# Hybrid mLSTM and attention layer, one core: x loaded between the first weight pieces, its squares between the weight copies, tile bursts issued in two parts, and u modulated and partly split on GpSimd

## What is computed

```python
mod = silu(cvec) @ w_ada + b_ada                 # cvec is c for latent tokens, c_ctx for the prompt
shift, scale, gate = split(mod, 3)               # each 2048 wide
u = rmsnorm(x, norm_pre_w) * (1 + scale) + shift
p = u @ w_in                                     # then attention, mLSTM, merge, output projection
```

## Time and profile before

| | us |
|---|---|
| median of 3 runs | 2286.16 (2285.41 to 2289.83) |
| the profiled execution, its own time | 2288.56 |
| span of the profiled execution | 2287.0 |
| TensorE busy, share of the span | 2138.0, 93% |
| VectorE busy | 875.2, 38% |
| ScalarE busy | 701.8, 31% |
| GpSimd busy | 105.2, 5% |
| end of the start (last matmul of the tiles steps) | 188.8 |

### The profile page before, as it was taken

The page is one execution under the profiler, slowest core; times in us unless marked ns, Lnnn a source line. Parts: engine busy times, 40 slices in busy tenths (PEclk is TensorE's granted clock), DMA queues, the critical chain, the costliest instruction groups (busy, mean ns, idle before and its releaser), DMA issues.

```text
span 2287.0 us, 34161 instructions
## 1 busy us (share of the span) xinstructions
PE 2138.0 (93%) x13450; PEld 1984.5 (87%) x13450; DVE 875.2 (38%) x1666; ACT 701.8 (31%) x1094; POOL 105.2 (5%) x184
## 2 busy tenths in 40 slices
PE   3898999899999999999999899999999899989995
PEld 1458999899999998999899899898989899977774
DVE  4775555432224233222322234342433533342223
ACT  4763111233233223322322223232323533331221
POOL 1001000000000000000000000000000100000000
PEclk7999999999999999999999999999999999999998
DMA  6873655542233223222422426243444534413223
GB/s 248 272 235 108 198 171 170 175 114 80 83 107 89 78 77 110 86 82 73 117 79 82 128 64 141 76 110 121 99 133 95 172 120 120 123 60 120 74 73 128
DMA packets 295167, 274.00 MB, mean 120 GB/s; under 512 B 17921, under 2 KB 243961, under 8 KB 292641
## 3 DMA queue, kind: packets, MB, share of 16 engines
q1 hardware_dynamic: 282416, 218.21, 33.6%
q0 software_dynamic: 12656, 54.40, 6.5%
HBM read 232.65 MB, written 39.92 MB: 119 GB/s over the span
## 4 chain that ended last, share of the span: by engine, by line
PE 83%; DVE 7%; issue 3%; ACT 2%; DMA 2%; SPq 1%; DVEq 0%; POOL 0%; ACTq 0%; POOLq 0%
PE bank L1374 60%; PE bank L1598 9%; PE bank L1463 2%; PE bank L1289 2%; PE bank L1345 2%; PE bank L1513 2%; PE bank L1328 1%; PE bank L1504 1%; DMA WORK<-in_state_n_dram 1%; PE bank L1515 1%; PE bank L1436 1%; DMA Y<-in_x_prompt_dram 1%; DVE WL L858 1%; DVE WL L876 1%; DVE XL L1246 1%
## 5 line engine op out<-in xcount | busy, mean ns | idle before, releaser
L1374 PE MATMUL bank<-XH,WH 128*128 128x320 f32 x3392 | 794.8, 316 | 41.1 <-DVE WL L858 30.0
L1374 PE MATMUL bank<-XH,WL 128*128 128x320 f32 x3392 | 777.8, 311 | 0.0
L1374 PE MATMUL bank<-XL,WH 128*128 128x320 f32 x3392 | 777.7, 311 | 0.0
L1374 PEld LDWEIGHTS bank<-XH,WH 128*128 128x128 f32 x3392 | 570.2, 190 | 52.7 <-DVE WL L858 29.7
L1374 PEld LDWEIGHTS bank<-XL,WH 128*128 128x128 f32 x3392 | 572.8, 190 | 0.0
L1374 PEld LDWEIGHTS bank<-XH,WL 128*128 128x128 f32 x3392 | 571.6, 189 | 0.0
L858 DVE TENSOR_TENSOR WL<-RAW,WH 128x1024 fp32r<-128x1024 f32 x244 | 298.4, 1224 | 606.7 <-ACT WH L618 605.2
L618 ACT ACTIVATE WH<-RAW 128x1024 fp32r<-128x1024 f32 x244 | 257.6, 1056 | 533.7 <-PE bank L1374 376.0
L628 ACT ACTIVATE OUTS<-bank 128x320 f32<-128x320 f32 x180 | 68.9, 434 | 477.6 <-PE bank L1374 477.6
L1598 PE MATMUL bank<-WH,XH 128*128 128x512 f32 x320 | 130.8, 409 | 13.8 <-ACT WORK L832 5.9
L1598 PE MATMUL bank<-WH,XL 128*128 128x512 f32 x320 | 126.6, 396 | 0.0
(11 more groups left out here) (198 smaller groups left out, 1651.3 us busy)
## 6 DMA issues: line engine op xcount, KB each, us to landing
RAW<-in_w_in_dram SPq DMA_DIRECT2D x180, 512.0 KB, 3.8
proj_dram<-OUTS POOLq DMA_DIRECT2D x92, 320.0 KB, 2.4
WORK<-in_w_ada_dram SPq DMA_DIRECT2D x54, 512.0 KB, 4.1
RAW<-in_w_ada_dram SPq DMA_DIRECT2D x42, 512.0 KB, 5.0
RAW<-in_w_out_dram SPq DMA_DIRECT2D x32, 512.0 KB, 3.7
WORK<-proj_dram SPq DMA_DIRECT2D x20, 640.0 KB, 4.6
WORK<-proj_dram POOLq DMA_DIRECT2D x32, 320.0 KB, 3.8
RAW<-in_w_proj_a_dram SPq DMA_DIRECT2D x16, 512.0 KB, 4.0
```

Of the source, the lines that this page charges most:

```text
L1374: ins = pe.matmul(banks[n][:, 0:HALF_TOK], w[:, k, :], x[:, k0 + k, n * HALF_TOK:(n + 1) * HALF_TOK], start=(first and k == 0 and wi == 0) ...
```

## The change

- **x block by block.** SP issues piece 0, x block 0, piece 1, x block 1, and so on to piece 4, x block 4, then the pieces from 5 on. Each block has a semaphore of its own.
- **Squares between the copies.** ScalarE squares block g right after it copied piece g (g = 0 to 4). VectorE computes mean + EPS at step 6 and scales one block in each of the steps 8 to 12.
- **Tile bursts in two parts.** A tiles step is issued by TensorE as part 0 (its first k-tile) and part 1 (its second). If an ada piece q = 0 follows, that piece goes between the parts (START_PE). START_DONE gives each step its place in TensorE's order of finishing, and the waits for weight slots and for a complete chunk count by it.
- **u on GpSimd for groups 0 to 2.** GpSimd modulates the twelve k-tiles (two tensor_scalar instructions each) and subtracts hi from u (one tensor_tensor of 640 each), in the order mod 0, mod 1, lo 0, mod 2, lo 1, mod 3, lo 2, lo 3. VectorE keeps the cast to hi. ScalarE no longer modulates these groups. Group 3 stays as it was: ScalarE modulates, VectorE casts and subtracts.

```diff
--- before.py
+++ after.py
@@ -54,6 +54,20 @@
     return START.index((kind, j, q))
 
 
+START_PE = []
+for _g, (_kind, _j, _q) in enumerate(START):
+    if _kind == "tiles":
+        START_PE += [(_g, 0), (_g, 1)]
+    elif _q == 0 and _g and START[_g - 1][0] == "tiles":
+        START_PE.insert(len(START_PE) - 1, (_g, None))
+    else:
+        START_PE.append((_g, None))
+START_DONE = {}
+for _g, _part in START_PE:
+    if _part != 0:
+        START_DONE[_g] = len(START_DONE) + 1
+
+
 def start_w(g):
 
     return g % START_W if g < N_START - 2 else g - (N_START - 2)
@@ -61,7 +75,7 @@
 
 def start_w_free(g):
 
-    return max((p for p in range(g) if start_w(p) == start_w(g)), default=-1) + 1
+    return max((START_DONE[p] for p in range(g) if start_w(p) == start_w(g)), default=0)
 
 
 def start_raw_count(g):
@@ -69,7 +83,7 @@
     return sum(16 if START[p][0] == "ada" else 32 for p in range(g % START_RAW, g + 1, START_RAW))
 
 
-WIDE_FREE = max(p for p in range(N_START) if start_w(p) >= 2) + 1
+WIDE_FREE = max(START_DONE[p] for p in range(N_START) if start_w(p) >= 2)
 
 
 C_IDENT, C_TRIF, C_TRIB, C_SEL, C_PERM, C_BAND, C_COS, C_SIN, C_END = 0, 128, 256, 384, 392, 520, 2056, 2568, 3080
@@ -266,7 +280,7 @@
         XT = OR
 
 
-        rows_in, const_in, x_in, aconst_in = sem("rows_in"), sem("const_in"), sem("x_in"), sem("aconst_in")
+        rows_in, const_in, x_in, aconst_in = sem("rows_in"), sem("const_in"), [sem(f"x_in{b}") for b in range(5)], sem("aconst_in")
         m0_in, mnull = sem("m0_in"), sem("mnull")
         raw_in = [sem(f"raw_in{i}") for i in range(4)]
         gada_in = [sem(f"gada_in{i}") for i in range(2)]
@@ -338,12 +352,11 @@
                     sp.dma_start(dst[:, :, 256:384], w_in_v[:, 2 * j:2 * j + 2, COL_SCAN:COL_SCAN + P])\
                         .then_inc(start_in[s], 16)
 
-            for g in range(4):
-                start_load(g)
             for b in range(5):
+                start_load(b)
                 src = x_sample[0, b * P:(b + 1) * P, :] if b < NB else x_prompt[0]
-                sp.dma_start(XT[:, b, :], src).then_inc(x_in, 16)
-            for g in range(4, N_START):
+                sp.dma_start(XT[:, b, :], src).then_inc(x_in[b], 16)
+            for g in range(5, N_START):
                 start_load(g)
 
             def w_half(g_base, g, slot, src, k=8):
@@ -513,6 +526,27 @@
                 pool.dma_start(GACC[0:1, v, :], b_ada[0:1, 4096:6144]).then_inc(gacc_init, 16)
 
 
+            def modulate(k):
+
+                pool.wait_ge(scl_done, k // 4 + 1)
+                pool.wait_ge(xt_out, 5 * (k // 4) + 5)
+                x = XTG[:, k % 4, :]
+                for v, cs in enumerate((slice(0, LAT), slice(LAT, TOK))):
+                    ins = nc.gpsimd.tensor_scalar(x[:, cs], x[:, cs], SCL[:, k, v:v + 1], MODS[:, k, v:v + 1],
+                                                  ALU.mult, ALU.add)
+                ins.then_inc(u_done, 1)
+
+            def low_u(k):
+                pool.wait_ge(u_hi, k + 1)
+                nc.gpsimd.tensor_tensor(XL[:, k, :], XTG[:, k % 4, :], XH[:, k, :].bitcast(F32),
+                                        ALU.subtract).then_inc(u_lo, 1)
+
+            for c in range(3):
+                modulate(4 * c)
+                for i in range(1, 4):
+                    modulate(4 * c + i)
+                    low_u(4 * c + i - 1)
+                low_u(4 * c + 3)
             pool.wait_ge(u_lo, KT)
             for a in (GI, GF, TA):
                 chain.link(nc.gpsimd.memset(a[0:100, :], 0.0))
@@ -680,23 +714,19 @@
 
             for g in range(N_START):
                 kind, j, q = START[g]
-                if g == 4:
-                    for b in range(5):
-                        act.wait_ge(x_in, 16 * 5)
-                        if b:
-                            act.wait_ge(sq_done, b)
-                        nc.scalar.activation(SQ, XT[:, b, :], ACT.Square, accum_out=SS[:, b:b + 1]).then_inc(sq_done, 1)
                 if g == N_START - 1:
                     for i in range(4):
                         modulate(3, i)
                 start_hi_part(g)
+                if g < 5:
+                    act.wait_ge(x_in[g], 16)
+                    if g:
+                        act.wait_ge(sq_done, g)
+                    nc.scalar.activation(SQ, XT[:, g, :], ACT.Square, accum_out=SS[:, g:g + 1]).then_inc(sq_done, 1)
                 for c in range(4):
                     for f in range(5):
                         if g == start_at("ada", 2 * c + 1, 2 + f) + 2:
                             transposed_x(c, f)
-                    for i in range(4):
-                        if c < 3 and g == start_at("ada", 2 * c + 2, 4 + i):
-                            modulate(c, i)
 
 
             hi(0, 0, 0)
@@ -878,7 +908,7 @@
 
             def mod_row(j):
 
-                dve.wait_ge(start_used, start_at("ada", j, 7) + 1)
+                dve.wait_ge(start_used, START_DONE[start_at("ada", j, 7)])
                 if j:
                     dve.wait_ge(ada_t, j)
                 V.tensor_copy(MR[0:4, :], bank[6][0:4, :]).then_inc(ada_row, 1)
@@ -905,16 +935,18 @@
                 if k >= 12:
                     dve.wait_ge(start_used, WIDE_FREE)
                 V.tensor_copy(XH[:, k, :], XTG[:, k % 4, :]).then_inc(u_hi, 1)
+                if k < 12:
+                    return
                 dve.wait_ge(u_hi, k + 1)
                 V.tensor_tensor(XL[:, k, :], XTG[:, k % 4, :], XH[:, k, :].bitcast(F32), ALU.subtract).then_inc(u_lo, 1)
 
             for g in range(N_START):
-                if g == 4:
+                if g == 6:
                     dve.wait_ge(sq_done, 5)
                     V.tensor_scalar(SS[:, :], SS[:, :], 1.0 / D, EPS, ALU.mult, ALU.add).then_inc(ms_done, 1)
-                if g == 5:
+                if 8 <= g < 13:
                     dve.wait_ge(rstd_done, 1)
-                    for b in range(5):
+                    for b in (g - 8,):
                         V.tensor_scalar(XT[:, b, :], XT[:, b, :], RSTD[:, b:b + 1], None, ALU.mult).then_inc(xn_done, 1)
                 if g == N_START - 1:
                     mod_row(7)
@@ -928,7 +960,7 @@
                     if j < 7 and g == start_at("ada", j + 1, 3):
                         mod_columns(j)
                 for k in range(12):
-                    if g == start_at("ada", 2 * (k // 4) + 2, 4 + k % 4) + 1:
+                    if g == start_at("ada", 2 * (k // 4) + 2, 5) + k % 4:
                         split_u(k)
 
 
@@ -1329,29 +1361,28 @@
                                         start=(kt == 0 and wi == 0), stop=(kt == KT - 1 and wi == 1))
                 ins.then_inc(start_used, 1)
 
-            def start_tiles(g, m):
+            def start_tiles(g, m, k):
 
                 pe.wait_ge(start_lo, g + 1)
                 wh, wl = start_wh[start_w(g)], start_wl[start_w(g)]
-                for k in range(2):
-                    kt = 2 * m + k
-                    if m == 5 and k == 1:
-                        mod_columns(7)
-                    pe.wait_ge(u_lo, kt + 1)
-                    for i in range(3):
-                        cs = slice(384 * k + P * i, 384 * k + P * i + P)
-                        for wi, (w, x) in enumerate(((wh, XH), (wh, XL), (wl, XH))):
-                            for n in range(2):
-                                ins = pe.matmul(bank[2 * i + n][:, 0:HALF_TOK], w[:, cs],
-                                                x[:, kt, n * HALF_TOK:(n + 1) * HALF_TOK],
-                                                start=(kt == 0 and wi == 0), stop=(kt == KT - 1 and wi == 2))
-                        if kt == KT - 1:
-                            ins.then_inc(tiles_done, 1)
-                if kt < KT - 1:
+                kt = 2 * m + k
+                if m == 5 and k == 1:
+                    mod_columns(7)
+                pe.wait_ge(u_lo, kt + 1)
+                for i in range(3):
+                    cs = slice(384 * k + P * i, 384 * k + P * i + P)
+                    for wi, (w, x) in enumerate(((wh, XH), (wh, XL), (wl, XH))):
+                        for n in range(2):
+                            ins = pe.matmul(bank[2 * i + n][:, 0:HALF_TOK], w[:, cs],
+                                            x[:, kt, n * HALF_TOK:(n + 1) * HALF_TOK],
+                                            start=(kt == 0 and wi == 0), stop=(kt == KT - 1 and wi == 2))
+                    if kt == KT - 1:
+                        ins.then_inc(tiles_done, 1)
+                if k == 1 and kt < KT - 1:
                     ins.then_inc(start_used, 1)
 
             pe.wait_ge(cs_done, 1)
-            for g in range(N_START):
+            for g, part in START_PE:
                 kind, j, q = START[g]
                 if kind == "ada":
                     mod_piece(g, j, q)
@@ -1360,7 +1391,7 @@
                     if j % 2 and 2 <= q < 7:
                         transposed_x(j // 2, q - 2)
                 else:
```

(2 more changed lines are left out.)

## The result

The changed kernel takes 2291.84 us (median; 2288.46 to 2297.59), against 2286.53 us (2285.23 to 2291.15) for the kernel before on the same chip: ratio 1.0017, 95% interval 1.0010 to 1.0025. That is 2.3 to 5.7 us slower, near the 0.2% that a measurement can tell from none; the forecast was 7 us faster. The profiled execution took 2297.59 us, its span 2296.0.

What follows compares the result with a forecast made beforehand. TensorE was busy 93% of the span, so gains were possible only where it idles: the start and three split windows. Start -8.8, windows +0.9, parts +1.0 sum to -6.9, giving 2279.3 us; own range 2275 to 2282.

Steps and rivals of the forecast that it cites:

- Start, first transposes 9.8 us earlier: Loading and scaling of x: first transposes at 46.3 instead of 56.1 us; -8.8 after a clock charge of 1.0.
- Low clock, +1.0: TensorE around the first transposes: pieces at 1.2 GHz cost 1.9 us, not 0.93; charged 1.0 against the start's gain.
- Split window, +0.3 each: From SCL to the even tile burst, three times: VectorE work 6.8 plus GpSimd waits 3.9, 10.7 against 10.4 us.
- The lone row of the prediction: Profile row before the change: a split ran 1.23 us beside GpSimd's power, unhindered; basis of a rival without exclusion.
- turns: Split windows: every GpSimd operation wins a turn against VectorE; window 12.8, sum +4.8, 2291 us; chance 0.17.
- the piece between the parts 1.8 late: Burst in two parts: piece q0 needs 4.6 us of VectorE work against 2.8 of part 0, +1.8 per window.
- Side by side: Split windows: only casts exclude GpSimd, each window shrinks by 3.6; sum -18.6, 2264 to 2268 us; chance 0.18.
- halfway: Split windows: subtractions steal some turns, a window costs about 2; sum -1.8, 2284 us; chance 0.23.
- Burst in parts, +1.0: Bursts in two parts: piece q3's weight slot comes free later, SCL 0.5 late in two windows, +1.0.

Runs made afterwards that it cites:

- x_only: Kernel before with only x loads, squares and scalings interleaved block by block; 2280.61 us, ratio 0.9963.
- x_clear_warm: x_only with squares in another tile, GACC cleared before x arrives, and eight unused matmuls ahead of the first transposes; 2278.04 us, ratio 0.9960.
- prices: Changed kernel plus three rounds of two scalings and a subtraction on GpSimd at the beginning; executed once for its trace, 2289.63 us.
- sub_pool: Changed kernel with whole bursts and modulation back on ScalarE, GpSimd only subtracting; 2281.81 us, ratio 0.9973 against before.
- mod_pool: Changed kernel with whole bursts and subtraction back on VectorE, GpSimd only modulating; 2289.09 us, ratio 1.0001 against before.
- x_pool: Changed kernel with whole tile bursts, u still on GpSimd; 2292.71 us, ratio 1.0015 against before.
- x_parts: Changed kernel without GpSimd's u work: modulation back on ScalarE, subtraction on VectorE, bursts in parts; 2282.02 us, ratio 0.9976 against before.

## Why the prediction was wrong

*Start, first transposes 9.8 us earlier:* right. Measured 9.3, and its steps with it: x landed at 25.6 (25.7 forecast), squares 1.91 us long with gaps between them, the last from 25.64 to 27.55 (27.8 forecast). Timeline of the changed kernel, GpSimd and VectorE:

```profile
30.08 2.03 POOL L521 TENSOR_TENSOR RSTD<-SS,HP 128x5 f32<-128x5 f32 x1 [23.96 <-DVE SS L946]
32.08 3.50 POOL L523 MEMSET WORK<- 128x4096 f32 x1
```

```profile
29.83 2.35 DVE L906 TENSOR_TENSOR XL<-RAW,XH 128x1024 fp32r<-128x1024 f32 x2
32.15 4.52 DVE L950 TENSOR_SCALAR Y<-Y,RSTD 128x2048 f32<-128x2048 f32 x1
```

The power took 2.03, not 1.20: it starts 0.25 us into two splits (29.83 to 32.18) and ends with them, at 32.11. I had its row of 2.12 in hand and used the other. Nothing came of it but a later clearing; the first scaling, blocked until 36.67, ends within 0.5 of the forecast's 36.2.

*Low clock, +1.0:* right in kind, too small. From the first transposes to SCL it took 14.5 instead of 12.1, +2.4; x_only has 1.6 of that, x_clear_warm takes 1.5 away with a clock of 1.00. The rows show the matmuls of a piece at 0.43 us spacing until about 51.6 in the changed kernel, and until 50.5 in x_only, and at 0.23 afterwards; why the clock rose later in the changed kernel no run shows, and GpSimd has no work there yet. With it the start gave 6.9 at SCL, not 8.8, and x_only's 6.8 at the marker is all that the change had to give.

*Split window, +0.3 each:* **the step that failed.** Its formula was 6.8 us of VectorE plus the durations of GpSimd's operations whose result VectorE waits for, 3 x 0.9 + 1.2. The window measured 12.5, +2.1. With the durations that prices measured, 3 x 1.22 + 1.56 = 5.2, the formula would have given 12.0, not 10.7: so 1.3 of the 1.8 us by which the window was missed can be put to the size of a term. I took the middle for a term that had nothing but bounds and counted nine times in the sum; the upper bounds, 1.3 and 1.75, give a window of 12.5 and a sum of -1.5, outside the range of my forecast, and I didn't work it out. (Two of the lower bounds are slips by their own rule: 0.75 for 0.73, and 0.65 for 0.55. Nothing hangs on them.)

The count was wrong too, and its errors offset each other. For sub_pool the formula gives 10.4 - 3 x 0.85 + 1.56 = 9.4, measured 10.8; for mod_pool 10.4 - 1.08 + 3 x 1.22 = 13.0, measured 12.2. The subtraction of the second tile, which I had left out, holds VectorE off as the first does, and the modulations cost VectorE less than their own time, since part of it passes beside its other work. The first window of the changed kernel, GpSimd and VectorE:

```profile
61.46 5.63 POOL L535 TENSOR_SCALAR WORK<-WORK,SCL,MODS 128x512 f32<-128x512 f32 x4 [24.19 <-DVE SCL L929]
67.06 1.55 POOL L541 TENSOR_TENSOR XL<-WORK,XH 128x640 fp32r<-128x640 f32 x1
68.61 2.48 POOL L535 TENSOR_SCALAR WORK<-WORK,SCL,MODS 128x512 f32<-128x512 f32 x2
71.05 1.54 POOL L541 TENSOR_TENSOR XL<-WORK,XH 128x640 fp32r<-128x640 f32 x1
```

```profile
61.26 2.35 DVE L906 TENSOR_TENSOR WL<-RAW,WH 128x1024 fp32r<-128x1024 f32 x2
64.64 0.50 DVE L937 CAST XH<-WORK 128x640 fp32r<-128x640 f32 x1 [1.03 <-POOL WORK L535]
65.06 1.71 DVE L906 TENSOR_TENSOR XL<-WORK,XH 128x1024 fp32r<-128x1024 f32 x1
67.12 1.84 DVE L937 CAST XH<-WORK 128x640 fp32r<-128x640 f32 x1 [0.35 <-POOL WORK L535]
68.88 1.21 DVE L906 TENSOR_TENSOR XL<-WORK,XH 128x1024 fp32r<-128x1024 f32 x1
71.12 1.83 DVE L937 CAST XH<-WORK 128x640 fp32r<-128x640 f32 x1 [1.02 <-POOL WORK L535]
72.86 0.94 DVE L906 TENSOR_TENSOR WL<-RAW,WH 128x768 fp32r<-128x768 f32 x1
...
76.59 1.21 DVE L906 TENSOR_TENSOR WL<-RAW,WH 128x1024 fp32r<-128x1024 f32 x1
```

The first modulation starts 0.20 us into two splits in a row and takes 3.15 instead of 1.22 (two of them 5.63). The third is issued while a cast already waits for the subtraction; that cast and the split at 68.88 go first, and it takes 2.48. Then GpSimd, free at last, starts the subtraction at 71.05 and holds off the cast at 71.12, 1.83 instead of 0.50, with the burst's weight split behind it. Read on VectorE: 2.4 of waiting for modulations, 0.5 in a stretched split, 2.7 in two stretched casts, 5.6 on top of the 6.8. The two engines alternate, and an operation on either is longer by part or all of the one that it meets. The lone row of the prediction, a split of 1.23 beside the power, misled as much as it said it might: that power was short. The Trainium skill ("SBUF — State Buffer", Who interferes with whom) states an exclusive lock between GpSimd and a VectorE instruction with two SBUF inputs or in a two-port mode, and whichever issues first gets it; the runs agree in both directions: GpSimd's 0.45 became 1.51 behind a split, and VectorE's splits of 1.22 became 1.71 here (2.31 in sub_pool) and its casts of 0.50 became 1.84 behind GpSimd.

*Rival "turns" (0.17):* nearest, in part by luck. It gave a window of 12.8 and 2291; measured 12.5 and 2291.84. It had right that both subtractions hold VectorE off and that splits are stretched; but with the durations of prices its four modulations and two subtractions make 14.8. Its other term, the piece between the parts 1.8 late, was there in kind and didn't show: the piece's split ends at 77.80 (the last row above), 3.9 us behind the start of the burst where 4.6 was forecast, and would have held up a first part of 2.6 by 1.3. The first part took 5.17, so the piece stands right behind it at 79.03 to 80.20, 1.17 instead of 0.93. What made it take so long is a term that I hadn't priced at all. *Side by side* fell with the stretched rows, *halfway* was some 6 us short (-1.8 against +4.1).

*The burst, in no term of the sum:* **the second step that failed, a cost put at nothing.** TensorE goes through the burst at a clock of 0.69, its first 18 matmuls in 5.17 instead of the 2.64 of the second part; before, the whole burst had 6.91 against 5.53, 1.4 of the kind. The three bursts with the piece between their parts take 3 x 8.98; before, they took 6.48 + 6.75 + 6.91 and a piece of 0.93 each: 26.9 against 22.9, **+4.0**. I had named the slow beginning only as something that "side by side" might win. That GpSimd's share in the work makes it worse is shown by x_pool against x_only (8.0 to 8.3 us a burst against 7.0); how slow one burst gets isn't foretold by its window alone, since the three of sub_pool took 5.55 to 7.42 behind windows of the same 10.8.

*Burst in parts, +1.0:* 0 at the marker (182.02 in x_parts, 182.04 in x_only), though the delay is where it was charged: in x_parts SCL comes 9.3 us behind the start of the odd burst in both cycles, in x_only 8.9, 0.4 for the 0.5 forecast. It is given back elsewhere, chiefly between an even burst and the next odd one (18.0, 17.9 and 17.9 us against 18.1, 18.1 and 18.2) and by an SCL 0.2 earlier in the first cycle. Beside GpSimd it isn't: the changed kernel ends 0.5 behind x_pool, which is most of the 0.7 below.

In sum: forecast -8.8 + 0.9 + 1.0 = -6.9; measured -6.9 + 6.3 for three windows + 4.0 for the bursts + 0.7 for the rest = +4.1. Of the 11.0 between the two, 1.9 lie in the start, 5.4 in the windows and 3.7 in the bursts and the rest, for which only +1.0 stood in the sum. I gave 0.6 to faster, chiefly because the window's cost was held to +0.3 by a price in the middle of its bounds and because the clock in the bursts had no price.

## What to carry to other kernels

In this kernel GpSimd was no second engine beside a VectorE that subtracts two SBUF operands or casts from SBUF to SBUF: an operation moved there costs its own time and waits for the split it meets, and takes turns back from VectorE. Ask where it stands in the chain that ends at the bound: at the head of it (the modulation) it cost 1.8 us a window, at its tail (the subtraction) 0.4. When a price has only bounds and is multiplied by nine, work out the result at both bounds before the sign is believed; and where the rows show the tensor engine slow behind idle stretches, a change that lengthens them needs a term for that too: it was 3.5 us here (x_pool against x_only), over half as much as the windows themselves. What did help was order alone: work that the next burst doesn't read moved out from ahead of it, and a clearing moved to where its engine is idle.

## What the runs showed of the hardware that I had not expected

- The waiting of a blocked operation is inside its duration, on both engines, and can be more than the work itself: a cast of 0.50 became 1.84, and eight GpSimd scalings that need 4.9 us filled 12.31 with no idle time in the record, so GpSimd looks like the bound where it mostly waits.
- GpSimd's scaling by two per-partition operands runs at 0.77 us for 512 and 0.45 for 128 elements: a fixed part of some 0.34, three times what I had assumed (0.1), so the 128-wide remainder costs over half of the 512-wide part.
- TensorE's granted clock fell inside the split window. Three rows of the changed kernel's TensorE timeline: the matmuls behind 2.06 us of idling still go at the high level (2.4 GHz, one each 0.23 us); the piece behind 2.24 more goes at the low one (1.2 GHz, one each 0.43), and the burst begins at that level.

```profile
66.82 0.39 PE L1360 MATMUL bank<-XH,CS 128*4 128x512 f32 x1 [2.06 <-DVE XL L906]
...
70.15 0.59 PE L1360 MATMUL bank<-XH,CS 128*4 128x512 f32 x1 [2.24 <-DVE XL L906]
70.53 0.63 PE L1360 MATMUL bank<-XL,CS 128*4 128x512 f32 x1
```
